# Loading the dense V tiles in halves of 512 columns, with a semaphore for each half

## The reference, cut to what matters

```python
def block(args):
    hb, ib, gb = args
    act = jax.nn.gelu(jnp.einsum('td,tkd->tk', hb, p['peer_u'][ib]))
    return jnp.einsum('tk,tkd->td', act * gb, p['peer_v'][ib])
...
h = layer_norm(DEEPNORM_ALPHA * h + gt2 * ffn, p['ln2_g'], p['ln2_b'])
```

## Time and profile before

| | us |
|---|---|
| median of 3 runs | 3394.62 |
| lowest, highest | 3393.59, 3398.86 |
| the profiled execution, its time | 3396.72 |
| the profiled execution, its span | 3395.0 |

### The profile page before, as it was taken

One profiled execution on the slowest core, in us unless ns is written; L12 is line 12 of the kernel. 1 busy time (PEld: TensorE's weight loads), 2 busy tenths in 40 slices (PEclk: granted clock), 3 DMA queues, 4 the chain that ended last, 5 costly groups with the idle time before them and its releaser, 6 DMA issues. The chain is left out here.

```text
span 3395.0 us, 36170 instructions
## 1 busy us (share of the span) xinstructions
PE 3168.5 (93%) x12774; PEld 2021.0 (60%) x12774; DVE 2055.7 (61%) x3562; ACT 651.2 (19%) x1206; POOL 1015.9 (30%) x622
## 2 busy tenths in 40 slices
PE   6999999999999999999999999889777778999996
PEld 2457666676757585877744444467666777444442
DVE  6544434444434344566675533688999997765667
ACT  2312122121212121211100000233333445100000
POOL 0011111020202020300000001266666664776675
PEclk8999999999999999999999999899888998999998
DMA  9764545445454536365464479699999998999997
GB/s 359 281 238 159 215 178 185 186 177 199 171 214 157 218 137 237 134 223 192 144 234 173 173 277 329 261 414 410 422 421 410 401 404 316 366 420 421 420 420 296
DMA packets 176745, 932.82 MB, mean 275 GB/s; under 512 B 24104, under 2 KB 38121, under 8 KB 94697
## 3 DMA queue, kind: packets, MB, share of 16 engines
q1 hardware_dynamic: 90778, 496.69, 39.1%
q0 software_dynamic: 73728, 402.69, 29.1%
q10 hardware_dynamic: 12112, 31.79, 2.4%
HBM read 908.81 MB, written 22.28 MB: 274 GB/s over the span
## 5 line engine op out<-in xcount | busy, mean ns | idle before, releaser
L1079 PE MATMUL ps<-mT,ring 128*128 128x256 f32 (+1 forms) x4096 | 1168.9, 446 | 1.1 <-PEq L216 1.1
L1079 PEld LDWEIGHTS ps<-mT,ring 128*128 128x128 f32 x4096 | 776.3, 190 | 386.8 <-issue 317.8
L711 POOL TENSOR_TENSOR dd<-mask_f,dt_g 128x1024 f32<-128x1024 f32 x16 | 30.3, 1896 | 933.0 <-DVE dt_g L981 932.4
L2853 PE MATMUL ps<-mT,turned_rows 128*128 128x128 f32 x2016 | 292.9, 299 | 16.6 <-ACT turned_rows L2347 15.8
L2262 POOL DMA_INDIRECT u_rows<-in_peer_u_dram,expert_indices x140 | 237.4, 1695 | 209.0 <-DVE expert_indices L2570 65.2
L2853 PEld LDWEIGHTS ps<-mT,turned_rows 128*128 128x128 f32 x2016 | 271.6, 211 | 31.4 <-issue 28.7
L2592 DVE CUSTOM_DVE_ANT_0 u_rows<-u_rows,yhy 128x2048 f32<-128x2048 f32 x106 | 239.8, 2288 | 27.6 <-DMA u_rows<-in_peer_u_dram,expert_indices 26.4
L871 DVE SCALAR_TENSOR_TENSOR conv<-ps,tap_g,conv 128x510 f32<-128x510 f32 (+1 forms) x48 | 33.8, 704 | 338.7 <-ACT conv L732 338.7
L2347 ACT COPY turned_rows<-ps 128x512 f32<-128x512 f32 x252 | 142.9, 586 | 400.0 <-PE ps L2845 399.7
L2653 DVE SCALAR_TENSOR_TENSOR turned_rows<-h_rows,expert_gate,turned_rows 128x1024 f32<-128x1024 f32 x124 | 159.6, 1290 | 80.4 <-DMA h_rows<-in_v_rest_dram,expert_indices 80.3
L2275 POOL DMA_INDIRECT h_rows<-in_v_rest_dram,expert_indices x130 | 176.6, 1358 | 95.6 <-DVE turned_rows L2653 55.3
(11 more groups left out here) (416 smaller groups left out, 4569.1 us busy)
## 6 DMA issues: line engine op xcount, KB each, us to landing
ring<-in_w_stream_dram SPq DMA_DIRECT2D x160, 1024.0 KB, 4.9
ada_tiles<-in_w_ada_dram SPq DMA_DIRECT2D x64, 1024.0 KB, 6.7
yhy<-in_v_dense_dram SPq DMA_DIRECT2D x128, 512.0 KB, 6.5
ring<-in_w_mix_dram SPq DMA_DIRECT2D x48, 1024.0 KB, 4.8
ring<-in_w_mod_dram SPq DMA_DIRECT2D x32, 1024.0 KB, 10.3
ring<-in_w_out_dram SPq DMA_DIRECT2D x32, 1024.0 KB, 7.2
rows<-cum_rows_scratch SPq DMA_DIRECT2D x16, 1536.0 KB, 12.9
ring<-in_w_q_dram SPq DMA_DIRECT2D x12, 1024.0 KB, 9.5
```

The costliest lines, as they stand in the source:

```text
L1079: mm = nc.tensor.matmul(ps[:, k % 4, 0:n], m.ring[:, slot, kt * P:(kt + 1) * P], m.mT[:, kt, 0:n], start=(kt == 0), stop=(kt == KT - 1))
L2853: mm = nc.tensor.matmul(ps[:, 2 + k % 2, 0:P], turned_rows[:, g, a * P:(a + 1) * P], m.mT[:, i, T + t * P:T + (t + 1) * P], start=(i == 0) ...
```

## The change

Each V tile is loaded by two DMAs of 512 columns, 256 KB each, 2 KB for each partition, and each half has its own semaphore; `vt_used` counts halves. TensorE does one half for both token tiles, then the other half for both. The last four tiles are still done for t = 0 first and for t = 1 after that. The wait of ScalarE is put into halves too and means the same moment.

```diff
-        vt_in = [sem(f"v_tile_{n}_loaded") for n in range(NVT)]
-        vt_used = sem("v_tiles_done")
+        vt_in = [sem(f"v_half_tile_{n}_loaded") for n in range(2 * NVT)]
+        vt_used = sem("v_half_tiles_done")
...
-                    if i >= NVT:
-                        sp.wait_ge(vt_used, i - NVT + 1)
-                    sp.dma_start(v_tile[:, i % NVT, :], d.v_dense[i]).then_inc(vt_in[i % NVT], 16)
+                    for k in range(2):
+                        n = 2 * i + k
+                        if i >= NVT:
+                            sp.wait_ge(vt_used, n - 2 * NVT + 1)
+                        sp.dma_start(v_tile[:, i % NVT, k * CH:(k + 1) * CH], d.v_dense[i][:, k * CH:(k + 1) * CH]).then_inc(vt_in[n % (2 * NVT)], 16)
...
-                act.wait_ge(vt_used, HALF)
+                act.wait_ge(vt_used, 2 * HALF)
...
-                def sum_tile(i, t):
-
-                    for k in range(2):
-                        mm = nc.tensor.matmul(ps[:, 2 * t + k, :], W[t][i // HALF][:, i % HALF, :], v_tile[:, i % NVT, k * CH:(k + 1) * CH],
-                                              start=(i == 0), stop=(i == NKEY - 1))
-                        if i == NKEY - 1:
-                            mm.then_inc(ffn_pe, 1)
-                    if t and i < NKEY - 1:
+                def sum_half(i, t, k):
+
+                    if not t:
+                        pe.wait_ge(vt_in[2 * (i % NVT) + k], 16 * (i // NVT) + 16)
+                    mm = nc.tensor.matmul(ps[:, 2 * t + k, :], W[t][i // HALF][:, i % HALF, :], v_tile[:, i % NVT, k * CH:(k + 1) * CH],
+                                          start=(i == 0), stop=(i == NKEY - 1))
+                    if i == NKEY - 1:
+                        mm.then_inc(ffn_pe, 1)
+                    elif t:
                         mm.then_inc(vt_used, 1)
...
-                for i in range(NKEY):
-                    pe.wait_ge(vt_in[i % NVT], 16 * (i // NVT) + 16)
-                    sum_tile(i, 0)
-                    if i < NKEY - NVT:
-                        sum_tile(i, 1)
-                for i in range(NKEY - NVT, NKEY):
-                    sum_tile(i, 1)
+                for i in range(NKEY - NVT):
+                    for k in range(2):
+                        for t in range(TT):
+                            sum_half(i, t, k)
+                for t in range(TT):
+                    for i in range(NKEY - NVT, NKEY):
+                        for k in range(2):
+                            sum_half(i, t, k)
```

## The result

| | before | changed |
|---|---|---|
| time, median | 3394.11 us | 3427.52 us |
| range of the runs | 3390.34 to 3398.86 (4) | 3422.9 to 3431.31 (4) |
| ratio, 95% interval | | 1.0097 [1.0085, 1.0109] |
| profiled execution, its span | 3396.72, 3395.0 us | 3431.31, 3429.6 us |

The change costs 33 us, 1.0%. The forecast was 3430 us. Between the two profiled executions the span grew by 34.6 us.

A forecast was written before the change was run, and what follows sets the result against it. PE and DMA engines both bound the kernel, gathers ending last. Lost turns slow tiles to 3.82 us; PE ends 38.3 us later, less 3.0 of room, 35.3 us, so 3430 us on the median's scale; range 3402 to 3465.

The forecast's parts named there:

- What bounds the kernel before: From 2950 to 3050 us PE and DMA engines are both full; gathers end last, PE has 3.0 us of room.
- TensorE's order, the semaphores, SyncE's second issue cost nothing: Same matmuls and weight loads, twice the waits unseen, SyncE's two issues 0.66 of 3.43 us a tile: no cost.
- 84 ns for a 2 KB piece: DMA engines' price by a line through three sizes; 81 ns more a tile, 9.7 us from 2912 us on.
- Turns packet by packet: Engines alternate queues whatever the packet size; half tile and gather take 1.912 us, a tile 3.82 against PE's 3.43.
- The sum: From 2912 us: gathers end at 3356, dense products at 3391.1, PE at 3411.7; VectorE's second L2677 starts 35.3 us later.
- Two terms of the sum: Crowded part from 2912 us: four gathers held back, leaving 226; ScalarE's loads add 12.0 us outside the one-to-one.
- The clock: PE stays at full clock, 2.4 GHz, in the stage though its share falls to 90%; nothing counted.
- A sign that failed: Expected in the crowded stage: PE busy about 90%, with some 200 waits for yhy of 0.2 us.
- (A): Rival, chance 0.12: two 2 KB pieces share a turn, PE stays fed, 3404 us; increments without a turn, 3405.
- (B): Rival, chance 0.05: dense loads lag within PE's 3.0 us room, gathers gain share, up to 3 us sooner, 3392.
- (C): Rival: a 2 KB piece costs 124 ns, giving 3500 us; chance 0.06 together with all over 3465.
- (D): Rival: PE still works tile by tile behind the second half; 3430 or up to 1.7 us more, within the 0.77.

The follow-up runs named there:

- section 2: Kernel before, still one DMA for each tile, but in 2 KB pieces: 3417.68 us, ratio 1.0066; in 1 KB pieces: 3537.26 us, ratio 1.0424.

## Why the prediction was right, step by step

- **What bounds the kernel before** (PE and the DMA engines both full, gathers last): borne out. Taking 120 of the gathers away gives no more than 14 us, because PE stands right behind them: its dense products then end at 3341.1 us instead of 3346.8, and its 12 rows, which took 26.5 us with waits for gathered rows in between, take 20.6.
- **TensorE's order, the semaphores, SyncE's second issue cost nothing**: shown, by the new order with whole tiles (1.0001) and by the old order with halves, whose interval overlaps the changed kernel's. For SyncE's second issue the run with halves and every second gather left out shows it: 0.9 us against whole tiles.
- **84 ns for a 2 KB piece**, not 124: 84 ns measured. The 9.7 us that the forecast counted for it aren't seen apart, since the gathers no longer end the kernel; in their place stands the pace of the pair.
- **Turns packet by packet**: 7582 to 7581. A half tile and a gather together took 100 us / 52.65 = 1.899 us (forecast 1.912), a tile 3.80 us (3.82). The shares add up to 103.5% where 102.6% was used, which is the difference. Equal counts in 100 us would also come of turns of several packets, equally many for each queue. The single packets in the trace exclude that: in these 100 us the end of a q0 packet meets, within 6 ns, 1.43 starts of q1's packets and 0.55 of q0's own on average, where chance gives 0.53 of each; the end of a q1 packet meets 1.43 of q0's and 0.49 of its own.
- **The sum**: no packet of q0 is left in the trace from 3353 to 3358 us (the row below), so the gathers of the crowded part had ended by about 3353 (3356); dense products until 3390.7 (3391.1); PE's end 3411.3 (3411.7); VectorE's second add 3411.36 (3411.7). The first add at 3397.62 follows PE's fourth of the 12 rows (3398.0 forecast), after 10.41 us of waiting for PE: VectorE's own path was not the bound.

```profile
q1 hardware_dynamic: 553, 1.01, 61.3%
```

- **Two terms of the sum.** The forecast held back four gathers until PE had finished the dense tiles; it was seven, as GpSimd issues in order. So 224 gathers ran in the crowd (32243 packets of q0 from 2912 to 3353 us) and not 226. That ends the gathers 3.8 us sooner, but PE's end moves by only a tenth of it, 0.4 us, since PE gets 90% of its pace in the crowd anyway. ScalarE's loads were counted as 12.0 us on top of the one-to-one. Until 3347 us (the rows below) q0 moved 222.7 gathers, which at 1.899 us are 422.8 of the 435 us; 12.2 are left, and q0 and q1 stayed one for one.

```profile
q0 software_dynamic: 32062, 116.74, 65.6%
q1 hardware_dynamic: 32055, 58.38, 34.9%
q10 hardware_dynamic: 576, 5.24, 2.8%
```

- **The clock**: the forecast counted nothing. It is 1.00 from 2950 to 3050 and from 3337 us until PE's last row, and 0.97 from 3148 to 3250 us, where ScalarE's loads took turns as well (row q10 below, 3148 to 3200 us) and PE waited up to 5.0 us at once. From 3152 to 3156 us the granted clock was 0.50, the lower of its two levels, 1.2 GHz, after PE had stood for 4.16 us before its products at 3148.64 us. Supply set the pace there too, so it cost nothing that shows in the sum.

```profile
q0 software_dynamic: 3342, 12.17, 57.2%
q1 hardware_dynamic: 3336, 6.08, 30.3%
q10 hardware_dynamic: 463, 3.39, 15.4%
```

- **A sign that failed**: "PE busy for about 90%, some 200 waits of 0.2 us". There are 206 and 7 waits, but PE's busy column stays at 100.00 and the waits are booked on the weight loads at 0.8 us each. The shortfall is in the counts (214 against 234, 91%). The step of the argument was right; the column I named for it was the wrong one.
- **The rivals.** (A), two pieces in a turn, or increments without a turn, at 3404: refuted by the packet counts in four forms of the load. The Trainium skill (DMA: Bandwidth & Descriptors, Queues, rings and completion order) says that an engine drains a whole packet of typically 9 to 17 descriptors from a queue before it changes. If that were its share of one DMA, a half tile and a gather (9 each) would still go one for one, but a tile's load of 17 in one DMA would take one turn and cost no more than the price of its pieces. The trace doesn't agree for these queues: 17 and 33 were counted one for one against 9 (section 2), and the ends and starts above show turns of a single packet. (B), a gain of share for the gathers: they did move 27.62 MB instead of 26.65 in 100 us, and ended earlier, but PE lost 0.37 us a tile. (C), 124 ns for a piece: refuted. (D), PE tile by tile behind the second half: the run with the old order, 2 us more, inside the noise.

## What to carry to other kernels

When two DMA queues both have work waiting, count the pieces and increments of each, not the bytes: a load in pieces of half the size moves half the bytes for each turn of the other queue, and even 64-byte transfers beside a large one take turns of their own. Before splitting a transfer to start compute earlier, look at whether the consumer waits for it at all (6.3 us here) and whether another queue is backed up; with the gathers thinned out the same split cost 0.9 us. A rate that an engine needs can be checked in one line: (turns of the load x mean turn of the other queue + its own time) against the consumer's period.

## What the runs showed of the hardware that was not expected

- Loads over 64 partitions made the 4 KB pieces of both queues take some 242 ns instead of 159, and the total fell to 278 GB/s with the engines' share at 103%. A full DMA row thus doesn't mean a full rate.
- With 2 KB gathers issued each 1.25 us, q1 got 720 packets in 100 us though the engines were only 0.75 busy, and the kernel with half the gathered bytes was 213 us slower. Its cause is open.
- With the same 2 KB pieces, 17 turns in one DMA gave 3417.7 us and 18 in two 3427.5: 10 us between kernels whose loads differ by 9 ns of engine time a tile. That it is the turn of the increment, and not the second DMA, fits the formula; no run separates them.
- A 1 MB load of two tiles beside the gathers needed 7.8 us to land, 4.7 at best, although its pieces have the largest share for each turn.

None of the versions that compute the whole reference was faster than the kernel before; the new order with whole tiles equals it.
